# Gate and query tiles of a decoder trunk in 512-column records summed by VectorE, with a second selection over 112 sums

## What is computed

```python
h = rmsnorm(x, attn_norm_gain[l])
q, k, v, pz, gu, gv, g = split(h @ w_in[l])
gates = sigmoid(g + b_gate[l])                      # 3 x 1024 columns
merged = gates0 * (attention @ w_branch_a) + gates1 * (pool @ w_branch_b) + gates2 * (gmlp @ w_branch_c)
x = x + merged @ w_out[l]
h2 = rmsnorm(x, ffn_norm_gain[l])
q = h2 @ w_query                                    # 8 heads x 2 halves x 128
v1, i1 = top_k(q[:, :, 0] @ keys1, 16); v2, i2 = top_k(q[:, :, 1] @ keys2, 16)
top, ci = top_k(v1[..., :, None] + v2[..., None, :], 16)       # 16 of 256 sums per head and token
idx = i1[ci // 16] * 128 + i2[ci % 16]
coeff = softmax(top) * gelu(h2 . expert_u[idx])
x = x + sum(coeff * expert_v[idx])
```

## Time and profile before

| | |
|---|---|
| median of 3 runs | 2029.03 us (2027.57 to 2030.46) |
| the profiled execution | 2028.88 us, span 2027.0 us |
| TensorE busy | 2004.3 us, 99% of the span |
| VectorE / ScalarE / GpSimd busy | 73% / 52% / 51% |
| TensorE's granted clock | 0.996 |

### The profile page before, as it was taken

One profiled execution on the slowest core, in us unless ns is written; L12 is line 12 of the kernel. 1 busy time (PEld: TensorE's weight loads), 2 busy tenths in 40 slices (PEclk: granted clock), 3 DMA queues, 4 the chain that ended last, 5 costly groups with the idle time before them and its releaser, 6 DMA issues.

```text
span 2027.0 us, 39960 instructions
## 1 busy us (share of the span) xinstructions
PE 2004.3 (99%) x12788; PEld 1819.2 (90%) x12788; DVE 1488.2 (73%) x3096; ACT 1061.8 (52%) x1746; POOL 1029.8 (51%) x425
## 2 busy tenths in 40 slices
PE   9999999999999999999999999999999999999998
PEld 7999998899999888888889999888999998888887
DVE  2855169988887888888639450799888878888886
ACT  5644555567776333333466444555677753333333
POOL 6898779787775000000278988798777740000001
PEclk8999999999999999999999999999999999999999
DMA  8355557675666787878774556676666567787775
GB/s 256 129 194 188 183 186 235 212 226 198 197 195 195 244 239 242 242 240 242 240 208 143 192 174 199 194 235 215 213 197 199 197 203 243 240 241 241 241 242 175
DMA packets 172128, 429.62 MB, mean 212 GB/s; under 512 B 19156, under 2 KB 83957, under 8 KB 171510
## 3 DMA queue, kind: packets, MB, share of 16 engines
q1 hardware_dynamic: 171588, 425.56, 66.5%
q10 hardware_dynamic: 434, 2.63, 0.3%
HBM read 392.79 MB, written 35.32 MB: 211 GB/s over the span
## 4 chain that ended last, share of the span: by engine, by line
PE 93%; DVE 3%; issue 1%; POOL 1%; ACT 1%; DMA 1%; DVEq 0%; POOLq 0%; ACTq 0%; SPq 0%
PE bank L1300 40%; PE bank L1563 33%; PE bank L1549 9%; PE bank L1551 5%; PE bank L1614 3%; POOL halves L545 1%; PE bank L1529 1%; DVE area L1155 0%; DVE area L1159 0%; DVE area L1162 0%; PE bank L1439 0%; DMA ring<-in_stream 0%; PE bank L1395 0%; DVE act L1235 0%; DMA x<-in_x 0%
## 5 line engine op out<-in xcount | busy, mean ns | idle before, releaser
L545 POOL TENSOR_TENSOR halves<-ring,halves 128x1024 fp32r<-128x1024 f32 x412 | 1024.2, 2498 | 975.7 <-DVE coef L1243 683.0
L626 ACT ACTIVATE halves<-ring 128x1024 fp32r<-128x1024 f32 x668 | 705.2, 1057 | 684.7 <-PE bank L1563 414.1
L1300 PE MATMUL bank<-hT,halves 128*128 128x256 f32 x6048 | 751.8, 283 | 1.9 <-DVE hT L921 1.7
L1300 PEld LDWEIGHTS bank<-hT,halves 128*128 128x128 f32 x6048 | 737.2, 192 | 4.4 <-DVE hT L921 2.1
L1563 PE MATMUL bank<-halves,coef 128*128 128x512 f32 x3000 | 681.5, 389 | 0.0
L1563 PEld LDWEIGHTS bank<-halves,coef 128*128 128x128 f32 x3000 | 562.7, 188 | 117.4 <-issue 0.5
L1223 DVE TENSOR_TENSOR halves<-ring,halves 128x1024 fp32r<-128x1024 f32 x256 | 315.5, 1233 | 12.7 <-ACT halves L626 10.2
L1549 PE MATMUL bank<-hT,halves 128*128 128x512 f32 x896 | 312.2, 395 | 3.0 <-POOL halves L545 3.0
L1551 PE MATMUL bank<-hT,halves 128*128 128x256 f32 x896 | 248.6, 277 | 0.0
L1549 PEld LDWEIGHTS bank<-hT,halves 128*128 128x128 f32 x896 | 168.1, 188 | 42.7 <-issue 3.6
L1551 PEld LDWEIGHTS bank<-hT,halves 128*128 128x128 f32 x896 | 168.3, 188 | 0.0
(11 more groups left out here) (168 smaller groups left out, 1375.0 us busy)
## 6 DMA issues: line engine op xcount, KB each, us to landing
ring<-in_stream SPq DMA_DIRECT2D x668, 512.0 KB, 4.0
held_blocks<-act SPq DMA_DIRECT2D x244, 128.0 KB, 1.8
act<-held_blocks SPq DMA_DIRECT2D x244, 128.0 KB, 3.0
area<-rel_scratch SPq DMA_DIRECT2D x16, 128.0 KB, 5.4
area<-in_gains SPq DMA_DIRECT2D x4, 512.0 KB, 4.1
x_home<-x ACTq DMA_DIRECT2D x2, 1024.0 KB, 4.2
x<-x_home SPq DMA_DIRECT2D x2, 1024.0 KB, 8.0
area<-in_params SPq DMA_DIRECT2D x2, 640.0 KB, 7.6
```

The source lines that it names most:

```text
L545: pool.tensor_tensor(halves[:, s, 1, :], ring[:, s, :], halves[:, s, 0, :].bitcast(F32), ALU.subtract)\
L626: a.activation(halves[:, s, 0, :], ring[:, s, :], ACT.Copy).then_inc(hi_done, 1)
L1300: i = pe.matmul(o, stationary[a], moving[b], start=begin and n == 0, stop=end and n == len(TERMS) - 1)
```

## The change

Gates 2 to 5 (16 tiles a layer) and the 16 query tiles go through `sided_columns`, one bank a tile. VectorE adds the two sides of each (`add_gates`, and 16 sums for the queries). ScalarE's sigmoid then works in place on the sum, in SBUF, once per tile; its copies of the queries fall away. Only the 112 sums that can be among the 16 best are formed (4 rows of 16, 12 rows of 4), with two additions a token tile instead of one; the rounds run over 112; the winner's row and column are now worked out with two shifts, three casts and four two-input operations. Folds stand less often in these rounds, so the selection ends at fold 45 where it ended at fold 52. ScalarE makes the high part of tile 48 before it waits for the exponential's input, and does `weighted(0)` before the last parked block; one fold stands between the first two `onehots`.

```diff
+PLAIN = 2
...
+WIDE = 4
+NARROW = 4
+CAND = WIDE * TOPK + (TOPK - WIDE) * NARROW
+assert (WIDE + 1) * (NARROW + 1) > TOPK and WIDE * TOPK == 64
...
-    + [(kind, "A" if kind == "gate" else "V") for kind, _ in MIX[1:] for _ in range(2)]
-    + [("wo", "V")] * 3 + [("h2T", "V")] * 2 + [("wo", "V")] + [("h2T", "V")] * 2 + [("qq", "A")] * 8 + [("score", "A")] * 8
+    + [step for kind, n in MIX[1:] for step in ([("branch", "V")] * 2 if kind == "branch" else [("gate", "A")] * 2 if n < PLAIN else [("sum", "V")] * 4)]
+    + [("wo", "V")] * 3 + [("h2T", "V")] * 2 + [("wo", "V")] + [("h2T", "V")] * 2 + [("qq", "V")] * 2 * PH + [("score", "A")] * 8
...
 
                     for k in range(2):
                         high_up_to(T_GATE[n] + 2 * k + 1 + 3)
-                        if n >= 3 and k == 0:
-                            a.wait_ge(taken_v, l * NGV + taken_before(place("branch", 2 * (n - 2) + 1) + 1)[0])
-                        b = group("gate")
+                        if n < PLAIN:
+                            b = group("gate")
                         for c in range(2):
                             hf, br = divmod(n, BR)
                             col = C_BGATE + br * KD + hf * 4 + 2 * k + c
-                            i = a.activation(sig_of(n)[:, 2 * k + c, :], b[:, c * S:(c + 1) * S], ACT.Sigmoid,
-                                             bias=par[:, col:col + 1])
-                        i.then_inc(taken_a, 1)
+                            into = sig_of(n)[:, 2 * k + c, :]
+                            if n >= PLAIN:
+                                a.wait_ge(taken_v, l * NGV + taken_before(place("sum", 4 * (n - PLAIN) + 2 * k + c) + 1)[0])
+                            i = a.activation(into, b[:, c * S:(c + 1) * S] if n < PLAIN else into, ACT.Sigmoid, bias=par[:, col:col + 1])
+                        i.then_inc(sig_done, 1) if n >= PLAIN else i.then_inc(taken_a, 1)
...
-                    b = group("qq")
-                    a.activation(qqT[:, h], b[:, :].rearrange("p (c t) -> p c t", c=2), ACT.Copy).then_inc(taken_a, 1)
...
                 with a.Fori(0, EXP_AT) as r:
                     for s in range(RING):
                         turn(r, s)
-                a.wait_ge(shifted_ready, l + 1)
-                a.activation(sel[:, 2], sel[:, 2], ACT.Exp).then_inc(gexp_ready, 1)
-                a.activation(stat[:, 13:14], one, ACT.Gelu_apprx_tanh)
-                with a.Fori(EXP_AT, PARKED // RING - 1) as r:
+                for r in range(EXP_AT, PARKED // RING - 1):
                     for s in range(RING):
-                        turn(r, s)
+                        if r == EXP_AT and s == 0:
+                            a.wait_ge(tiles_used, l * NT + r * RING + (T_PU + s + 1))
+                            high(r * RING + (T_PU + RING + s), s)
+                            a.wait_ge(shifted_ready, l + 1)
+                            a.activation(sel[:, 2], sel[:, 2], ACT.Exp).then_inc(gexp_ready, 1)
+                            a.activation(stat[:, 13:14], one, ACT.Gelu_apprx_tanh)
+                            park(r, s)
+                        else:
+                            turn(r, s)
...
+                    if s == RING - 1:
+                        weighted(0)
...
-                a.wait_ge(weights_hi, 2 * l + 2)
-                weighted(0)
                 for n in range(SETS):
+                    if n == 1:
+                        a.wait_ge(act_done, l * NK + PARKED)
...
+                def add_gates(n):
+
+                    if n >= 3:
+                        v.wait_ge(taken_v, l * NGV + taken_before(place("branch", 2 * (n - 2) + 1) + 1)[0])
+                    for k in range(4):
+                        b = group("sum")
+                        v.tensor_reduce(sig_of(n)[:, k, :], b[:, :].rearrange("p (e t) -> p t e", e=2), AX.X, ALU.add)\
+                            .then_inc(taken_v, 1)
+
                 for hf in range(2):
                     for br in range(BR):
+                        if PLAIN <= 3 * hf + br + 1 < 2 * BR:
+                            add_gates(3 * hf + br + 1)
...
+                g[0] = first("qq")
+                for n in range(2 * PH):
+                    b = group("qq")
+                    v.tensor_reduce(qqT[:, n // 2, n % 2, :], b[:, :].rearrange("p (e t) -> p t e", e=2), AX.X, ALU.add)\
+                        .then_inc(taken_v, 1)
...
                 for t in range(TT):
                     fold()
-                    i = v.tensor_tensor(cand[:, t], val[:, t, :, 0, :].unsqueeze(3).to_broadcast([P, PH, TOPK, TOPK]),
-                                        val[:, t, :, 1, :].unsqueeze(2).to_broadcast([P, PH, TOPK, TOPK]), ALU.add)
+                    for a0, many, width, at in ((0, WIDE, TOPK, 0), (WIDE, TOPK - WIDE, NARROW, WIDE * TOPK)):
+                        sums = cand[:, t, :, at:at + many * width].rearrange("p h (a b) -> p h a b", a=many)
+                        i = v.tensor_tensor(sums, val[:, t, :, 0, a0:a0 + many].unsqueeze(3).to_broadcast([P, PH, many, width]),
+                                            val[:, t, :, 1, 0:width].unsqueeze(2).to_broadcast([P, PH, many, width]), ALU.add)
                 then_search(i)
                 fold()
                 pairs = [(t, h) for t in range(TT) for h in range(PH)]
                 for k in range(2):
                     ks = slice(8 * k, 8 * k + 8)
-                    flat = [cand[:, t, h].rearrange("p a b -> p (a b)") for t, h in pairs]
+                    flat = [cand[:, t, h, :] for t, h in pairs]
                     for n, ((t, h), f) in enumerate(zip(pairs, flat)):
                         i = v.max(top[:, t, h, ks], f)
                         if n < len(pairs) - 1:
-                            fold_every(6, n)
+                            fold_every(8, n)
...
-                v.tensor_scalar(ca.rearrange("p t h j -> p (t h j)"), ci.rearrange("p t h j -> p (t h j)"), 4, None,
-                                ALU.logical_shift_right)
-                link(v.tensor_scalar(cb.rearrange("p t h j -> p (t h j)"), ci.rearrange("p t h j -> p (t h j)"), 15, None,
-                                     ALU.bitwise_and))
-                v.tensor_copy(caf.rearrange("p t h r -> p (t h r)"), ca.rearrange("p t h r -> p (t h r)"))
-                link(v.tensor_copy(cbf.rearrange("p t h r -> p (t h r)"), cb.rearrange("p t h r -> p (t h r)")))
+                flat = [z.rearrange("p t h j -> p (t h j)") for z in (ci, ca, cb)]
+                v.tensor_scalar(flat[1], flat[0], 4, None, ALU.logical_shift_right)
+                link(v.tensor_scalar(flat[2], flat[0], 2, None, ALU.logical_shift_right))
+                v.tensor_copy(row_of, flat[1])
+                v.tensor_copy(quarter, flat[2])
+                link(v.tensor_copy(column, flat[0]))
+                fold()
+                link(v.scalar_tensor_tensor(flat_a, quarter, float(WIDE - WIDE * TOPK // NARROW), row_of, ALU.add, ALU.max))
+                v.scalar_tensor_tensor(row_of, flat_a, -float(TOPK), column, ALU.mult, ALU.add)
+                link(v.scalar_tensor_tensor(quarter, flat_a, -float(NARROW), column, ALU.mult, ALU.add))
+                link(v.scalar_tensor_tensor(flat_b, quarter, float(WIDE * NARROW - WIDE * TOPK), row_of, ALU.add, ALU.max))
...
-                while folds[0] < PARKED:
+                while folds[0] < PARKED - 1:
...
                 onehots(0)
+                fold()
...
+                def sided_columns(n, o, second=None):
+
+                    w = tile(n, KD)
+                    for k in range(KD):
+                        if second is not None and k == KD // 2:
+                            pe.wait_ge(taken_v, second)
+                        one = pe.matmul(o[:, :].rearrange("p (e t) -> p e t", e=2), w[:, 0, k], hT[:, :, k], start=k == 0, stop=False,
+                                        skip_group_check=True)
+                        i = pe.matmul(o[:, 0:S], w[:, 1, k], hT[:, 0, k], start=False, stop=True, skip_group_check=True)
                         if k == 0:
                             one.then_inc(tiles_used, 1)
                     return i
...
-                for h in range(PH):
+                for n in range(2 * PH):
                     b = group("qq")
-                    if h == 0:
+                    if n == 0:
                         pe.wait_ge(taken_v, rows_ready("h2T", 3))
-                    for c in range(2):
-                        i = columns(T_WQ + 2 * h + c, b[:, c * S:(c + 1) * S], rows_ready("h2T", 4) if h + c == 0 else None)
-                    i.then_inc(groups_done, 1)
+                    sided_columns(T_WQ + n, b, rows_ready("h2T", 4) if n == 0 else None).then_inc(groups_done, 1)
                 for n in range(8):
                     b = group("score")
                     if n < 4:
-                        pe.wait_ge(taken_a, l * NGA + taken_before(first("qq") + 2 * n + 2)[1])
```

(23 more changed lines are left out.)

30 lines of the change are left out of this document (21 added, 9 removed).

## The result

The changed kernel takes 2033.68 us (median of 20 runs, 2029.99 to 2041.92), the kernel before 2029.02 (20 runs, 2026.98 to 2032.84): a ratio of 1.0024, interval 1.0018 to 1.0031. The forecast was 2030.6 in a range of 2017 to 2036. The profiled execution of the changed kernel took 2034.57 us, its span is 2032.6, against 2028.88 and 2027.0. One execution of a kernel of the experiments (`e5_spaced`) took 11307 us and is in no comparison.

What follows compares the result with a forecast made beforehand. TensorE, busy 2004.3 of 2027.0 us, was taken as the bound. Gates and queries -2.5, selection +3.5 us a layer, doubled +2.0, taken as +1.7: 2030.6 us, range 2017 to 2036.

Steps and rivals of the forecast that it cites:

- Sums, lock and folds: Second selection: lock waits on GpSimd make fold 33 10 us late, fold 44 11.6; block 49 loses 6.9 us.
- The allowance of 6.1 us: Parked stage: a fold may start up to 6.1 us late without TensorE waiting; lateness beyond that is waited out.
- Held stage and one-hots: Held stage starts 4.5 us later, one-hots win back 1.0: selection +3.5 us a layer.
- Tiles in two records: Gate and query tiles: 32 go from 2.88 to 2.773 us each, -3.4 us a layer.
- the pace of blocks 48 to 53: Slower pace, 2.84 us a tile, as the lower end for the two-record tiles: -1.3 us a layer.
- The wait at branch 3: Gate stage: second tile of branch 3 ready at 160.4, wanted at 160.0; +0.5 us a layer, bounds 0 and +2.3.
- The give-back before the queries: Final splits before the output projection follow GpSimd's beat and give back +0.4 us a layer, bounds 0 to 1.
- The sum: Whole kernel: 2 x (-2.5 + 3.5) = +2.0 us, taken as +1.7: 2030.6 us, 1.6 over the median.
- VectorE keeps up: Rival, chance 0.28: one lock wait instead of five, folds within 6.1 us; selection -3.3 a layer, 2017.3 us.
- The records bring nothing: Rival, chance 0.06: each two-record tile keeps its 2.88 us for another reason; 2035.6 us.

Runs made afterwards that it cites:

- e5_spaced: Changed kernel with three more folds in the 112-sum rounds (after every 5 maxima and every 6 replacements of the first round): 2025.70 us, ratio 0.9975.
- e6_both: Changed kernel with operands of the second selection's additions, subtractions, shifts and casts in PSUM banks, and three more folds in its rounds: 2022.75 us, ratio 0.9962.
- e7_early: e6_both with the exponential at block 36 instead of block 44: 2023.77 us, ratio 0.9958.
- e8_wide: Kernel before with gate and query tiles in two records, its old 256-sum selection kept but with operands in PSUM banks: 2026.97 us, ratio 0.9975.
- e12_exp: Changed kernel with the exponential again ahead of the high part in block 44: parked stage 159.53 and 159.62 us in one execution.
- e3_dense: Changed kernel with folds in the 112-sum rounds as dense as in the kernel before, eight more: 2039.69 us, ratio 1.0040.

## Why the prediction was right, and where not

*Sums, lock and folds: right, step by step.* With 1.41 us taken off, fold 21 starts at 329.85 (said: 329.85), fold 23 at 339.59 (339.9), fold 31 at 362.66 (362.8), fold 33 at 372.91 (373.1), fold 44 at 405.03 (405.2), block 49 at 411.29 (411.4). The allowance of 6.1 us held from block 38 on: fold 33 is 9.8 us late and block 38 has lost 3.6. At blocks 36 and 37 TensorE waits for the bank that folds 32 and 33 free, a second limit that my count left out; it changed nothing at the end. One part of the split was off: I had put two lock waits of 1.5 and 2.3 us among subtractions, shifts and casts; the rows show 1.63 us for the subtractions, some 1.2 of it waiting, and 2.49 for the first cast, some 2.2 of it waiting: 3.4 in sum against 3.8. The Trainium skill's rule of the port pair (SBUF — State Buffer, section SBUF: two separate sides) names two SBUF inputs or a two-port mode as what takes the lock; the trace agrees: a pair of additions takes 3.48 and 5.02 us within SBUF, 1.15 with one input in a bank.

*Held stage and one-hots: right.* Said +4.5 and -1.0. From the first parked block to the first held one it takes 163.01 us against 158.70, +4.3, and from there to the one-hots 2.87 against 3.91, -1.0. Layer 1 has +4.2 and -1.0.

*Tiles in two records: right in size for this execution's queries, wrong for the gates.* The term took 2.773 us a tile for both. The query tiles had it (-1.68), and that is in part luck: 16 of the 24 query stages in two records ran 0.84 us slower. The gate tiles ran at 2.83, 2.82, 2.83 us in every run, so their 16 won 0.85 us, not 1.7. The lower end that I named, the pace of blocks 48 to 53, is what they have. The Trainium skill's isolated gap (TensorE: Matmul & The Clock Gate, section Back-to-back issue gap) would have given less still; the trace differs from it, with 347 or 353 ns a chunk.

*The wait at branch 3: half the size.* Said +0.5, measured 0.22: the branch behind gate 4 takes 6.14 us instead of 5.92, as the last sums start behind the split, which did shorten to 0.69 us. Timelines of DVE and of PE, as the earlier trace rows:

```profile
156.63 0.69 DVE L925 TENSOR_TENSOR merged_halves<-area,merged_halves 128x512 fp32r<-128x512 f32 x1
157.24 1.88 DVE L1051 TENSOR_REDUCE area<-bank 128x256 f32<-128x512 f32 x3
```

```profile
159.62 6.14 PE L1343 MATMUL bank<-attn_halves,halves 128*128 128x256 f32 x48
```

*The give-back before the queries: the step that failed.* Said +0.4, bounds 0 and 1. It is 0.36 in layer 1 and 1.87 in layer 0, above the bound. I looked only at the splits before the projection. The bigger price is paid behind it: L946 reads two SBUF inputs, so it can lose to a subtraction of GpSimd that starts 0.03 us behind it, and the pair takes 3.62 us instead of 1.4. None of the six layers with gates in three records had this, twelve of the 22 others did. That the gates' records bring it about is likely by these counts; what decides the race isn't shown.

*The sum.* Said +1.0 us a layer; measured +2.72 and +1.13, of which the give-back is 1.5 in layer 0. The other 1.86 us lie ahead of gate 1 and differ from kernel to kernel. By the medians the change costs 4.7 us where I had said 1.6: the direction and the selection's mechanism are right, the size is nearly three times mine, and the result is in the part of the range (slower by over 4 us) that had a chance of 0.25. Misses also cancel in part in each layer: the gates' tiles won 0.85 us less than said, but the wait at branch 3 cost 0.3 less and the selection 0.2. *VectorE keeps up*, the rival with 0.28, is what `e6_both` shows once the lock is gone and three folds are moved in: -3.7 us a layer in the selection, where I had said -3.3. *The records bring nothing* is out for the queries.

## What to carry to other kernels

An operation of VectorE with two SBUF inputs, or a cast or shift within SBUF, can cost a whole subtraction of GpSimd, however small it is (a cast of 256 elements took 2.49 us instead of 0.28); splitting one into two gives it a second chance to wait. Put one operand in a free PSUM bank before making it smaller. Work put between the folds of a paced stage must leave each of them within what the ring allows: shorter work with its folds in the wrong place lost what the same work won with three folds moved.

## What the runs showed that was not expected

**Two paces of one loop.** Windows of `e7_early`, parked stage of layer 0 and of layer 1 (stretch, us, busy time of PE, number of instructions, granted clock, DMA share, GB/s):

```profile
267.99:417.84 149.85, 149.85 (x867) 1.00 0.69 226
1269.39:1422.11 152.72, 152.72 (x867) 1.00 0.69 224
```

The same code, the full granted clock, no wait, and 2.87 us apart. In the first every block takes 2.773 us (347 ns a chunk), in the second they take 2.830, 2.831 and 2.819 in turn (353 ns). A stage keeps its pace until something makes it wait; behind the wait it can be the other one, either way. Three of 28 parked stages ran slow from the start, 16 of 24 query stages in two records, and all 22 gate stages in two records. The three-record tiles never did: 92.34 us in all six gate stages without the change. So the profiled execution of the changed kernel, with both query stages fast, is 1.7 us better there than most. What sets the pace wasn't tried.

**A clock that drops for one tile.** In layer 1 of `e5_spaced` the first query tile takes 4.42 us instead of about 2.9. Windows, before it and in it (busy time of PE, weight loads, DVE, ACT and POOL, granted clock, DMA share, GB/s):

```profile
1212.00:1216.90 4.90, 3.27 (x18) 2.21 (x16) 4.05 (x8) 2.44 (x7) 1.60 (x1) 1.00 0.59 214
...
1218.00:1220.40 2.40, 2.40 (x9) 2.01 (x9) 0.00 (x0) 0.60 (x1) 2.40 (x2) 0.50 0.65 259
```

The granted clock falls from 1.00 to 0.50 (2.4 to 1.2 GHz) behind a stretch in which PE was busy for 3.27 of 4.90 us. The same tile, 4.42 us long, stands in one layer of `e7_early` and one of `e8_wide`: 3 of 24, some 1.5 us each. The falls in `e12_exp` and `e3_dense` above came behind single waits of 3.02 and 4.97 us, in both layers of each. No wait of 1.61 us or less in the parked stages had one behind it. Together with the two paces and the race this may be why the runs of these kernels lie further apart (12 us for the changed kernel, 6 for the one before); how often each occurs in the runs without a profile can't be read.
